# Down projections of a two-layer trunk on one core: shared sums left in PSUM, ScalarE's and the loads' order changed, GpSimd's weight remainders in operations of 256 columns

## Chip, core and metric

One core of one Trainium2 chip. The time is device microseconds of one execution; the kernel before takes 2417.88 us, the median of three runs (2416.55 to 2417.92).

## What is computed

A causal decoder trunk of two layers runs one step over 1024 prompt tokens and 32 sample tokens (1056 columns; activations lie feature by token, 128 features to a tile). Each layer has a mixer (convolution and dilated attention in layer 0, short convolution and spatial gating in layer 1) and a feed-forward part. Only that part is touched:

```python
gu = h @ P['ffn_w_gate_up'][layer]
x = x + mod[:, 5] * ((jax.nn.silu(gu[..., :FFN_HIDDEN]) * gu[..., FFN_HIDDEN:]) @ P['ffn_w_down'][layer])
```

`D_MODEL` is 1024 and `FFN_HIDDEN` 2816, which is eleven groups of 256 hidden features.

## The kernel before

**Operands in two words.** Every float32 operand is split into a high and a low part (`hi`, `lo`, fp32r), and a product is three matmuls: high by high, high by low, low by high. ScalarE makes the high words with a copy, GpSimd the low ones with a subtraction (`raw - hi`), a quarter of a slot of 2048 columns at a time.

**Seven products.** The gate and up projections and most of the down projection are done as 2 by 2 block products with seven multiplications in place of eight. Sums of the blocks are therefore needed of the weights (VectorE, `weight_sums` L2334 to L2340, `words_summed` L2371 to L2376) and of the activations, and the seven products have to be combined afterwards.

**Gate and up (`ffn`, items `split`, `w_split`, `products`).** For each group the gate, then the up unit. ScalarE splits the raw weights (`part_hi`, L1821) and then their sums (`sums_hi`, L1827, one copy of 2048 columns); GpSimd follows with `part_lo` and `sums_lo` (L3075), both waiting on the semaphore `part_hi_done`. During an up unit ScalarE's next work behind `sums_hi` is two copies of product 1 to `f_sum` (`copy_p1`, L1837), for which TensorE waits before it adds the next product into the same bank. What the down projection needs of a group (hidden features and four sums of their blocks) is written to a scratch tensor in HBM.

**Down (`piece_products` L3428, `piece_leaves`).** Group 10 goes first in the plain way, group 9 last (`down_blocks`, L3563), and groups 0 to 8 in five chunks of 1, 2, 2, 2, 2 groups (`CHUNKS`). A chunk has four pieces (one for each pair of output tiles, `m`), a piece two steps (one for each pair of token blocks, `PAIRS`), a step seven products, and a product three matmuls of 264 columns for each group: 21 matmuls a step in chunk 0, 42 in the others. That is 20 pieces a layer. The products of a step lie in four of six PSUM banks (`chain_bank`): chain 0 holds P1, then C11; chain 1 P5, then C12; chain 2 P7, then C21; chain 3 P6. VectorE takes them out in the order P1, P5, P7, P6, C11, C12, C21, and `piece_left` counts these events by seven for each step. P1 + P6 is the shared sum: it is kept in `u_acc` in SBUF over all chunks. In chunk 0 ScalarE copies P1 there (`copy_shared`, L1885), and TensorE waits for that copy (`u_copied`) before product 5, which overwrites the bank; in the other chunks VectorE adds P1 to it (L2414). VectorE adds P6 (L2423). P5 and P7 go straight to x (L2381; L2383 and L2384 for the block that ends in the sample tokens). In the last chunk the whole shared sum is added to x in three places by `add_shared`, half a piece later, reading `u_acc` and x, both in SBUF.

**What feeds a piece.** Each piece has its weights of the chunk's groups (`words`) and their block sums (`word_sums`). In every engine's program order, piece p is preceded by `piece_load` of piece p + 2 (SyncE, L1447), by `piece_words` of piece p + 1 and by one load of an operand of the next chunk (`f_load`, `load_operands`, L1465 to L1468, four of them with `i` = 0 to 3 for two groups, high and low words). `piece_words` is `words_summed` on VectorE, `words_hi` on ScalarE (L1891 for the words, L1893 for the sums) and `words_lo` on GpSimd (L3106, L3108, each one subtraction of 512 columns in chunk 0 and of 1024 in the others). TensorE waits on `word_lo` before products 1 and 2, and at the first piece of a chunk on the operands' loads.

The order of the queues in a piece (`ffn`, from L634):

```python
items.append(Item("piece_load", of=made[p + 2]) if p + 2 < PIECES else Item("last_load", layer=layer, k=p))
...
items.append(Item("piece_words", of=made[p + 1]))
...
elif 0 < piece.chunk < len(CHUNKS) - 1:
    items.append(Item("f_load", layer=layer, chunk=piece.chunk + 1, i=piece.m))
...
items.append(piece)
```

## Time and profile before

| | |
|---|---|
| median of three runs | 2417.88 us |
| the profiled execution, its own time | 2419.25 us |
| its span | 2417.5 us |
| TensorE matmul busy | 2327.5 us (96%) |
| VectorE, ScalarE, GpSimd busy | 1531.6, 799.3, 891.6 us |
| mean granted TensorE clock | 0.991 |
| groups 0 to 8 of the down projection | 1085.33 to 1288.64 us (layer 0), 2167.50 to 2371.92 us (layer 1) |

Busy times of engines are unions of their instructions. PE is TensorE's matmuls and PEld its weight loads; a matmul is recorded with its whole passage, so that consecutive ones overlap, and the distance of their starts is what one costs. DVE is VectorE, ACT ScalarE, POOL GpSimd. "Idle before" is an engine's idle time just ahead of an instruction, with what ended it. A stretch has its start and end, its length, the busy time and number of instructions of PE, PEld, DVE, ACT and POOL, the granted TensorE clock, the DMA engines' busy share and GB/s.

### The profile page before, as it was taken

Reading aid. Unit: us, or ns where it says so; the run is one execution under the profiler, and the core shown is the slowest. Engines: PE = TensorE matmul, PEld = TensorE weight load, DVE = VectorE, ACT = ScalarE, POOL = GpSimd, SP = SyncE. Lnnn points to the kernel's source line nnn. Section 1 sums busy time; section 2 is a strip of 40 time slices with the busy share of each in tenths; the row PEclk is TensorE's granted clock in tenths of the full one; section 3 lists DMA queues with packets and bytes.
Section 4 is the critical chain, followed back from the end, with each engine's and each line's share of the span. In section 5 each row is a group of like instructions: output and inputs, shape, how many; then the busy total and the mean of one; then the engine's idle time right before and its main releaser. Section 6 shows DMA issues by size and latency. Waiting matters only on the chain.

```text
span 2417.5 us, 42723 instructions
## 1 busy us (share of the span) xinstructions
PE 2327.5 (96%) x17575; PEld 2203.9 (91%) x17575; DVE 1531.6 (63%) x3075; ACT 799.3 (33%) x1250; POOL 891.6 (37%) x666
## 2 busy tenths in 40 slices
PE   7999999999999999999999999999999999999998
PEld 5997888588999999998998999999999999999997
DVE  5367743567766766758788320546766666658787
ACT  5212334425433333312214212144533333312113
POOL 3221111213445444534443432132545555424440
PEclk9999999999999999999999999999999999999999
DMA  9424343872456455465651688311334353565651
GB/s 306 168 68 146 114 147 99 291 240 86 142 192 238 162 179 195 153 266 206 237 192 53 217 298 284 114 37 36 134 109 170 114 179 116 187 260 199 227 181 73
DMA packets 220158, 411.70 MB, mean 170 GB/s; under 512 B 9588, under 2 KB 200329, under 8 KB 207934
## 3 DMA queue, kind: packets, MB, share of 16 engines
q1 hardware_dynamic: 206058, 328.53, 39.3%
q0 software_dynamic: 5648, 76.29, 9.0%
q10 hardware_dynamic: 8260, 4.15, 0.6%
q8 instruction: 141, 2.31, 0.4%
q14 instruction: 51, 0.42, 0.1%
HBM read 309.14 MB, written 143.64 MB: 187 GB/s over the span
## 4 chain that ended last, share of the span: by engine, by line
PE 67%; DVE 6%; DMA 2%; ACT 2%; issue 2%; SPq 0%; POOL 0%; ACTq 0%; DVEq 0%
PE ps L3297 15%; PE ps L3428 12%; PE ps L3326 10%; PE ps L3328 9%; PE ps L3327 9%; PE ps L3563 4%; PE ps L3517 3%; DVE x L2381 2%; DMA fa_lo<-scratch_f 1%; DMA w_raw<-in_ffn_w_gate_up 1%; PE ps L3698 1%; PE ps L3586 1%; DMA fb_lo_end<-scratch_f 0%; PE ps L3410 0%; DMA cache_v<-in_cache_b_kv 0%
## 5 line engine op out<-in xcount | busy, mean ns | idle before, releaser
L3297 PE MATMUL ps<-h_hi,w_slot 128*128 128x352 f32 x2112 | 538.0, 328 | 2.9 <-DVE acc_s L2272 1.4
L3297 PEld LDWEIGHTS ps<-h_hi,w_slot 128*128 128x128 f32 x2112 | 370.6, 188 | 22.0 <-issue 18.7
L3326 PE MATMUL ps<-h_hi,w_slot 128*128 128x264 f32 x1280 | 367.1, 287 | 3.9 <-ACT f_sum L1837 2.8
L3327 PE MATMUL ps<-h_lo,w_slot 128*128 128x264 f32 x1280 | 363.6, 284 | 0.0
L3328 PE MATMUL ps<-h_hi,w_slot 128*128 128x264 f32 x1280 | 362.3, 283 | 0.0
L3052 POOL TENSOR_TENSOR w_slot<-w_raw,w_slot 128x512 fp32r<-128x512 f32 x132 | 177.6, 1373 | 482.5 <-ACT w_slot L1655 473.7
L3297 PE MATMUL ps<-h_lo,w_slot 128*128 128x352 f32 x1056 | 339.4, 321 | 0.0
L3075 POOL TENSOR_TENSOR w_slot<-w_sum,w_slot 128x512 fp32r<-128x512 f32 x160 | 221.1, 1414 | 267.6 <-ACT w_slot L1827 267.6
L3066 POOL TENSOR_TENSOR w_slot<-w_raw,w_slot 128x512 fp32r<-128x512 f32 x168 | 226.9, 1384 | 187.0 <-DVE w_sum L2340 99.9
L3326 PE MATMUL ps<-t_hi,w_slot 128*128 128x264 f32 x960 | 274.2, 286 | 0.1
L3328 PE MATMUL ps<-t_hi,w_slot 128*128 128x264 f32 x960 | 272.7, 284 | 0.0
L3327 PE MATMUL ps<-t_low,w_slot 128*128 128x264 f32 x960 | 272.7, 284 | 0.0
L3326 PEld LDWEIGHTS ps<-h_hi,w_slot 128*128 128x128 f32 x1280 | 240.3, 188 | 10.9 <-ACT f_sum L1837 5.3
L3328 PEld LDWEIGHTS ps<-h_hi,w_slot 128*128 128x128 f32 x1280 | 241.2, 188 | 0.0
L3327 PEld LDWEIGHTS ps<-h_lo,w_slot 128*128 128x128 f32 x1280 | 240.7, 188 | 0.0
L3297 PEld LDWEIGHTS ps<-h_lo,w_slot 128*128 128x128 f32 x1056 | 199.5, 189 | 0.1
L3428 PE MATMUL ps<-fa_hi,p_hi 128*128 128x264 f32 x560 | 164.4, 294 | 25.9 <-ACT u_acc L1885 12.0
L3326 PEld LDWEIGHTS ps<-t_hi,w_slot 128*128 128x128 f32 x960 | 180.5, 188 | 5.3 <-issue 4.9
L3328 PEld LDWEIGHTS ps<-t_hi,w_slot 128*128 128x128 f32 x960 | 180.7, 188 | 0.0
L3327 PEld LDWEIGHTS ps<-t_low,w_slot 128*128 128x128 f32 x960 | 180.4, 188 | 0.0
L3106 POOL TENSOR_TENSOR p_lo<-p_raw,p_hi 128x1024 fp32r<-128x1024 f32 (+1 forms) x40 | 87.2, 2180 | 251.3 <-DVE p_raw L2376 251.3
L2381 DVE SCALAR_TENSOR_TENSOR x<-ps,mod,x 128x264 f32<-128x264 f32 x280 | 134.6, 490 | 46.2 <-PE ps L3428 44.3
(460 smaller groups left out, 5181.0 us busy)
## 6 DMA issues: line engine op xcount, KB each, us to landing
w_raw<-in_ada_w SPq DMA_DIRECT2D x48, 1024.0 KB, 6.0
w_raw<-in_ffn_w_gate_up SPq DMA_DIRECT2D x44, 1024.0 KB, 5.2
out_kv_sample<-in_cache_b_kv POOLq DMA_DIRECT2D x8, 4088.0 KB, 22.6
scratch_f<-ft_hi SPq DMA_DIRECT2D x18, 1056.0 KB, 8.6
scratch_f<-ft_lo SPq DMA_DIRECT2D x18, 1056.0 KB, 10.3
fa_hi<-scratch_f SPq DMA_DIRECT2D x10, 1848.0 KB
fa_lo<-scratch_f SPq DMA_DIRECT2D x10, 1848.0 KB
p_raw<-in_ffn_w_down SPq DMA_DIRECT2D x72, 256.0 KB, 3.0
```

Of the source, the lines that this page charges most:

```text
L2381: return dve.scalar_tensor_tensor(x[:, m, c], src, gate, x[:, m, c], ALU.mult, ALU.add)
L3052: pool.tensor_tensor(lo_of(u)[:, c], w_raw[raw_of[u].slot][:, c], hi_of(u).bitcast(F32)[:, c], ALU.subtract)\
L3066: pool.tensor_tensor(w_slot[slot_of(it.raw)][:, c], w_raw[it.raw.slot][:, c], w_slot[it.hi[0]].bitcast(F32)[:, c], ALU.subtract).then_inc( ...
L3075: pool.tensor_tensor(w_slot[it.sums[0]][:, c], whole[:, c], w_slot[it.sums_hi[0]].bitcast(F32)[:, c], ALU.subtract).then_inc(part_made, 1)
L3106: pool.tensor_tensor(p_lo[a][:, c], p_raw[a][:, c], p_hi[a].bitcast(F32)[:, c], ALU.subtract).then_inc(word_lo, 1)
L3297: mm = pe.matmul(big(t)[:, b, 0:BLK], wt, xt[:, k, b * BLK:b * BLK + BLK], start=(k == 0 and n == 0), stop=(k == K - 1 and n == 2))
L3326: pe.matmul(bank(it, j), w_high, x_high, start=first, stop=False, skip_group_check=True)
L3327: pe.matmul(bank(it, j), w_high, x_low, start=False, stop=False, skip_group_check=True)
L3328: return pe.matmul(bank(it, j), w_low, x_high, start=False, stop=last, skip_group_check=True)
L3428: mm = pe.matmul(ps[:, chain_bank(step, chain), 0:QB], w, xt, start=(start and u == 0 and n == 0), stop=(u == U - 1 and n == 2), skip_grou ...
L3517: return pe.matmul(big(t + m)[:, b, 0:BLK], halves[s][:, k, m * P:m * P + P], xt[:, k, b * BLK:b * BLK + BLK], start=(k == 0 and step == 0 ...
L3563: mm = pe.matmul(big(t + i)[:, bank, 0:BLK], halves[s][:, k, m * P:m * P + P], xt[:, k, c], start=(k == 0 and n == 0), stop=(k == 1 and n ...
```

## The change

- In the last chunk VectorE writes P1 + P6 back to the PSUM bank of chain 3 and adds it to x from there in three places, between C11 and C12 of the same step, with two waits on its own earlier results. `add_shared` is gone. The bank is free for TensorE after C12 rather than after P6, and the first tile of `down_blocks` waits for the last of these additions (`u_added`).
- ScalarE in chunk 0: `words_hi` of piece p + 1 stands between the two `copy_shared` of piece p, not ahead of both.
- ScalarE, sums of gate and up weights: two copies of 1024 columns; for an up unit the second stands behind the two copies of product 1. GpSimd's `sums_lo` waits for each half.
- Operand loads of chunks 2 to 4: both of the first group with piece 0 of the chunk before, the third with piece 1, the fourth with piece 2.
- `words_lo` on GpSimd: operations of 256 columns.

```diff
@@ make_plan, ffn
             items.append(Item("products", of=up, which=0))
+            items.append(Item("w_split_rest", of=up))
...
             elif 0 < piece.chunk < len(CHUNKS) - 1:
-                items.append(Item("f_load", layer=layer, chunk=piece.chunk + 1, i=piece.m))
+                for i in ((0, 1), (2,), (3,), ())[piece.m]:
+                    items.append(Item("f_load", layer=layer, chunk=piece.chunk + 1, i=i))
@@ chain_before
-                        return piece_left, 7 * back + LAST_LEFT[other]
+                        in_last = back % (2 * PIECES) >= 2 * (PIECES - 4)
+                        return piece_left, 7 * back + (C12_LEFT if in_last and other == 3 else LAST_LEFT[other])
@@ ScalarE
-                act.activation(w_slot[it.hi[0]], w_raw[it.raw.slot], ACT.Copy).then_inc(part_hi_done, 1)
-
-            def sums_hi(it):
-
+                act.activation(w_slot[it.hi[0]], w_raw[it.raw.slot], ACT.Copy).then_inc(part_hi_done, 2)
+
+            def sums_hi(it, half):
+
+                c = slice(1024 * half, 1024 * half + 1024)
                 act.wait_ge(sums_made, 4 * it.n + 4)
                 act.wait_ge(*it.sums_hi[1])
-                act.activation(w_slot[it.sums_hi[0]], w_sum[it.sums[0]].rearrange("p s k n -> p (s k n)"), ACT.Copy)\
+                act.activation(w_slot[it.sums_hi[0]][:, c], w_sum[it.sums[0]].rearrange("p s k n -> p (s k n)")[:, c], ACT.Copy)\
                     .then_inc(part_hi_done, 1)
...
+            def copy_shared(it, i):
+
+                step = 2 * it.n + i
+                act.wait_ge(piece_done, 7 * step + P1_LEFT)
+                act.activation(u_acc[:, it.m, HALF[PAIRS[i]]], ps[:, chain_bank(step, 0), 0:QB], ACT.Copy).then_inc(u_copied, 1)
...
                 elif it.kind == "w_split":
-                    sums_hi(it.of)
+                    sums_hi(it.of, 0)
+                    if it.of.role == "f_gate":
+                        sums_hi(it.of, 1)
+                elif it.kind == "w_split_rest":
+                    sums_hi(it.of, 1)
...
                 elif it.kind == "piece_words":
-                    words_hi(it.of)
+                    if it.of.k not in range(1, 5):
+                        words_hi(it.of)
                 elif it.kind == "piece":
                     if it.chunk == 0:
-                        copy_shared(it)
+                        copy_shared(it, 0)
+                        words_hi(pieces_of[it.layer][it.k + 1])
+                        copy_shared(it, 1)
@@ VectorE, piece_leaves
-                    dve.tensor_tensor(u, four, u, ALU.add).then_inc(piece_left, 1)
-                    if last and i:
-                        add_shared(it, PAIRS[0])
-                    elif last and it.m:
-                        add_shared(pieces_of[it.layer][it.k - 1], PAIRS[1])
+                    dve.tensor_tensor(four if last else u, four, u, ALU.add).then_inc(piece_left, 1)
                     done(C11_LEFT)
                     add_to_x(m0, B0[r], one_, g0).then_inc(piece_left, 1)
+                    if last:
+                        made(P6_LEFT)
+                        add_to_x(m1, B1[r], four, g1)
+                        add_to_x(m0, B1[r], four, g0)
+                        add_to_x(m1, B0[r], four, g1).then_inc(u_added, 1)
+                        dve.wait_ge(u_added, 8 * it.layer + 2 * it.m + i + 1)
                     done(C12_LEFT)
...
-                if last and it.m == 3:
-                    add_shared(it, PAIRS[1])
@@ GpSimd
-                pool.wait_ge(part_hi_done, it.r + 1)
+                pool.wait_ge(part_hi_done, 2 * it.r + 2)
...
                 for q in range(4):
+                    if q % 2 == 0:
+                        pool.wait_ge(part_hi_done, 2 * it.rs + 1 + q // 2)
...
                 pool.wait_ge(word_sums, 4 * it.n + 4)
-                pool.tensor_tensor(p_lo[a][:, c], p_raw[a][:, c], p_hi[a].bitcast(F32)[:, c], ALU.subtract).then_inc(word_lo, 1)
-                pool.wait_ge(word_hi, 2 * it.n + 2)
-                pool.tensor_tensor(p_lo[b][:, c], p_raw[b][:, c], p_hi[b].bitcast(F32)[:, c], ALU.subtract).then_inc(word_lo, 1)
+                for n, w in enumerate((a, b)):
+                    pool.wait_ge(word_hi, 2 * it.n + 1 + n)
+                    for q in range(2 * len(it.units)):
+                        d = slice(256 * q, 256 * q + 256)
+                        low = pool.tensor_tensor(p_lo[w][:, d], p_raw[w][:, d], p_hi[w].bitcast(F32)[:, d], ALU.subtract)
+                    low.then_inc(word_lo, 1)
@@ TensorE, down_blocks
-                    if it.of.src == "hidden" and i < 2:
-                        pe.wait_ge(piece_left, 7 * (2 * PIECES * (it.of.layer + 1) - 1) + (7 if i else P6_LEFT))
+                    if it.of.src == "hidden" and i == 0:
+                        pe.wait_ge(u_added, 8 * (it.of.layer + 1))
+                    elif it.of.src == "hidden" and i == 1:
+                        pe.wait_ge(piece_left, 14 * PIECES * (it.of.layer + 1))
```

## Rows read from the trace of the kernel before

**Rows 1.** The page: busy time by engine, and the chain that ended last.

```profile
PE 2327.5 (96%) x17575; PEld 2203.9 (91%) x17575; DVE 1531.6 (63%) x3075; ACT 799.3 (33%) x1250; POOL 891.6 (37%) x666
...
PE 67%; DVE 6%; DMA 2%; ACT 2%; issue 2%; SPq 0%; POOL 0%; ACTq 0%; DVEq 0%
```

**Rows 2.** Waits of TensorE's weight loads, whole run: us in total, times, longest.

```profile
PEld ps L3428 <- ACT u_acc L1885: 13.7, 8, 2.5
PEld ps L3428 <- DVE x L2381: 11.9, 6, 2.1
...
PEld ps L3326 <- ACT f_sum L1837: 5.3, 12, 0.4
```

**Rows 3.** Stretches (columns above): chunk 0, chunks 1 to 3, last chunk; then layer 1.

```profile
1085.33:1115.35 30.02, 23.46 (x170) 22.41 (x169) 25.89 (x77) 8.57 (x16) 12.30 (x8) 0.94 0.49 179
1115.35:1239.86 124.51, 123.48 (x1010) 122.97 (x1009) 96.58 (x257) 25.49 (x24) 57.21 (x24) 1.00 0.66 234
1239.86:1288.64 48.78, 43.60 (x337) 42.97 (x338) 44.63 (x106) 8.72 (x8) 21.06 (x12) 0.97 0.32 110
2167.50:2199.10 31.60, 24.94 (x171) 23.89 (x169) 26.48 (x78) 8.56 (x16) 12.27 (x8) 0.89 0.47 171
...
2324.19:2371.92 47.73, 42.24 (x340) 41.40 (x339) 44.98 (x108) 8.71 (x8) 21.10 (x12) 1.00 0.25 91
```

**Rows 4.** The chain that ended last, down projections: start us, us, what.

```profile
1111.53 117.08 PE ps L3428 x954
1229.56 10.26 DMA fa_lo<-scratch_f
...
2273.72 9.38 DMA fb_lo_end<-scratch_f
```

**Rows 5.** Timeline of VectorE and GpSimd in the last chunk of layer 0.

```profile
1254.40 4.05 DVE L2381 SCALAR_TENSOR_TENSOR x<-u_acc,mod,x 128x264 f32<-128x264 f32 x3
...
1288.49 1.29 DVE L2381 SCALAR_TENSOR_TENSOR x<-ps,mod,x 128x264 f32<-128x264 f32 x3
1289.82 1.30 DVE L2381 SCALAR_TENSOR_TENSOR x<-u_acc,mod,x 128x264 f32<-128x264 f32 x3
...
1252.82 2.41 POOL L3106 TENSOR_TENSOR p_lo<-p_raw,p_hi 128x1024 fp32r<-128x1024 f32 x1 [7.09 <-DVE p_raw L2376]
1255.19 2.57 POOL L3108 TENSOR_TENSOR p_lo<-p_raw,p_hi 128x1024 fp32r<-128x1024 f32 x1
```

**Rows 6.** Timeline of ScalarE, VectorE and GpSimd in chunk 0 of layer 0.

```profile
1110.14 1.06 ACT L1893 ACTIVATE p_hi<-p_raw 128x1024 fp32r<-128x1024 f32 x1 [3.21 <-DVE p_raw L2376]
1111.11 0.37 ACT L1885 ACTIVATE u_acc<-ps 128x264 f32<-128x264 f32 x1
...
1109.68 0.43 DVE L2376 TENSOR_TENSOR p_raw<-p_raw,p_raw 128x256 f32<-128x256 f32 x1
...
1110.26 2.38 POOL L3106 TENSOR_TENSOR p_lo<-p_raw,p_hi 128x1024 fp32r<-128x1024 f32 x1 [4.76 <-DVE p_raw L2376]
1112.59 2.41 POOL L3108 TENSOR_TENSOR p_lo<-p_raw,p_hi 128x1024 fp32r<-128x1024 f32 x1
```

**Rows 7.** Groups of GpSimd's subtractions by form: busy us, mean ns of one.

```profile
L3108 POOL TENSOR_TENSOR p_lo<-p_raw,p_hi 128x1024 fp32r<-128x1024 f32 x32 | 77.6, 2425 | 0.0
...
L3108 POOL TENSOR_TENSOR p_lo<-p_raw,p_hi 128x512 fp32r<-128x512 f32 x8 | 10.3, 1287 | 0.0
```

**Rows 8.** Stretch with three operand loads under way (columns as in rows 3).

```profile
1062.00:1082.00 20.00, 19.25 (x118) 18.93 (x119) 12.06 (x28) 2.69 (x5) 2.54 (x2) 1.00 0.87 367
```

**Rows 9.** Timeline of ScalarE and GpSimd in an up unit of layer 1.

```profile
1955.23 1.90 ACT L1827 ACTIVATE w_slot<-w_sum 128x2048 fp32r<-128x2048 f32 x1
1957.04 0.65 ACT L1837 ACTIVATE f_sum<-ps 128x264 f32<-128x264 f32 x2
...
1957.21 5.22 POOL L3075 TENSOR_TENSOR w_slot<-w_sum,w_slot 128x512 fp32r<-128x512 f32 x4 [5.39 <-ACT w_slot L1827]
```

**Rows 10.** A stretch of chunk 0 in layer 1 (columns as in rows 3).

```profile
2171.30:2174.70 3.40, 3.40 (x16) 3.40 (x17) 1.89 (x6) 0.64 (x2) 1.50 (x2) 0.50 0.92 381
```

More of the change, by code:

```diff
@@ L1878, in up_products @@
                             copy_gate_p1(sevens["f_gate", it.layer, it.j + 1], m)
-            def copy_shared(it):
-                for i, r in enumerate(PAIRS):
-                    step = 2 * it.n + i
-                    act.wait_ge(piece_done, 7 * step + P1_LEFT)
-                    act.activation(u_acc[:, it.m, HALF[r]], ps[:, chain_bank(step, 0), 0:QB], ACT.Copy).then_inc(u_copied, 1)
+            def copy_shared(it, i):
+                step = 2 * it.n + i
+                act.wait_ge(piece_done, 7 * step + P1_LEFT)
+                act.activation(u_acc[:, it.m, HALF[PAIRS[i]]], ps[:, chain_bank(step, 0), 0:QB], ACT.Copy).then_inc(u_copied, 1)
             def words_hi(it):
@@ L2384, in add_to_x @@
                 return dve.tensor_tensor(acc_s[:, m, :], src[:, n:n + S_TOK], acc_s[:, m, :], ALU.add)
-            def add_shared(it, r):
-                u = u_acc[:, it.m, HALF[r]]
-                g0, g1 = [mod[:, 6 * it.layer + it.gate, m, 0:1] for m in (2 * it.m, 2 * it.m + 1)]
-                dve.wait_ge(piece_left, 7 * (2 * it.n + PAIRS.index(r)) + C21_LEFT)
-                add_to_x(2 * it.m, B1[r], u, g0)
-                add_to_x(2 * it.m + 1, B1[r], u, g1)
-                add_to_x(2 * it.m + 1, B0[r], u, g1).then_inc(u_added, 1)
             def piece_leaves(it):
@@ L3101, in words_lo @@
             def words_lo(it):
-                a, b, c = it.words[0], it.word_sums[0], slice(0, 512 * len(it.units))
-                pool.wait_ge(word_hi, 2 * it.n + 1)
+                a, b = it.words[0], it.word_sums[0]
                 pool.wait_ge(word_sums, 4 * it.n + 4)
-                pool.tensor_tensor(p_lo[a][:, c], p_raw[a][:, c], p_hi[a].bitcast(F32)[:, c], ALU.subtract).then_inc(word_lo, 1)
-                pool.wait_ge(word_hi, 2 * it.n + 2)
-                pool.tensor_tensor(p_lo[b][:, c], p_raw[b][:, c], p_hi[b].bitcast(F32)[:, c], ALU.subtract).then_inc(word_lo, 1)
+                for n, w in enumerate((a, b)):
[4 more added lines that the diff above has]
+                    low.then_inc(word_lo, 1)
             moved = [0]
```

1 line of the change is left out of this document (removed).

## Prediction, made before the changed kernel was timed

> **What bounds the kernel.** I read the page first. TensorE's matmuls are busy 96% of the span and hold 67% of the chain that ended last [rows 1]. So an edit pays only where TensorE itself waits, and the next view is the list of its waits [rows 2]. Three of the longest are in the lines of this change: product 5 of chunk 0 waits for ScalarE's copy of P1 (13.7 us, 8 times), steps of the last chunk wait for VectorE's additions to x (11.9 us, 6 times), and the up units wait for ScalarE's copy to `f_sum` (5.3 us, 12 times).
>
> A list of waits counts some idle time that is no loss, so I measure against distances. Undisturbed, 954 matmuls of L3428 take 117.08 us [rows 4], 0.1227 us each with two short waits inside; I use 0.122. A step of 42 matmuls is then 5.12 us, a two-group piece 10.25, a one-group piece 5.12. The stretches [rows 3] say where more is taken. Chunks 1 to 3 are nearly clean (124.51 us for 1008 matmuls, which make 123.0). Chunk 0 has 168 matmuls, 20.5 us, and takes 30.02 and 31.60. The last chunk has 336, 41.0 us, and takes 48.78 and 47.73. These stages are where the time lies.
>
> **1. Shared sum in PSUM, last chunk.** Three additions of `u_acc` to x take 4.05 us while GpSimd's two subtractions of 1024 columns run, and 1.30 us when GpSimd is idle [rows 5]. The last of the three ends 0.7 us behind GpSimd: additions with both inputs in SBUF stand still beside it. Additions to x from PSUM do not: three take 1.29 us [rows 5]. There are three such groups in each layer, and three TensorE waits of 1.8 to 2.1 us behind them. With the source in PSUM I expect none of it, that is 7.8 us back in layer 0 (48.78 less 41.0) and 6.7 in layer 1, 14.5 in all; 1.5 of layer 0's is the lower clock behind such a wait (granted 0.97 over 48.78 us [rows 3]).
>
> What is put in: the same number of additions, now all between C11 and C12. The write of P1 + P6 goes to PSUM, which no row shows; I take the 0.43 us it has now. The wait for P6 is hidden by C11. The wait on `u_added` lets one addition end before the next starts, 0.49 in place of 0.40 us: 0.09 a step. VectorE's work in the chunk: 44.6 us busy [rows 3], less three groups of about 2.8 us standing still (8.8 with the longer third), plus the group of 1.3 us that now falls behind the end, plus eight waits of 0.09 = 37.8 us, against TensorE's 41.0. It fits, but not in every step. From a step's start, by 0.73 us a product and 0.2 until VectorE begins: P6 is in `four` at 3.5, C11 added at 4.25, the shared sum at 5.5, C12 and C21 at 6.3. Then come the next piece's four block sums (0.43 us each, some 0.36 in a row [rows 6]) until 7.8, and P1, which TensorE needs at 5.12 + 2.93 = 8.05, has left at about 8.2: 0.2 us, three times a layer, 1.2 in all. The bank of chain 3, now free after C12, is asked for more than a step later: no cost, and still none if C12 came 2 us late. The first tile of L3563 wants the last three additions at 5.12 and gets them at about 5.6: 0.5 a layer, 1.0 in all. With 0.3 for rests, the part gives **12.0 us**.
>
> The Trainium skill, VectorE: DVE Perf Modes, section "The TRN2 errata — SBUF-src ops pay a fixed extra latency per instruction", gives VectorE 58 cycles and the columns for an SBUF source and 120 for a PSUM source, at 0.96 GHz: 65 ns more for each addition that now reads PSUM. By that 48 additions would cost 3.1 us of VectorE, and this part would give about 10. The trace disagrees: 1.29 us for three from PSUM, 1.30 for three from SBUF.
>
> **2. ScalarE's order in chunk 0.** ScalarE does the high words of the next piece's sums, which wait for VectorE, before it copies P1: in piece 3, 1.06 us, and TensorE is held until 1111.5 [rows 6]. The copy needs only P1. With it ahead, that wait goes; the second copy has the words between (2 x 0.6 us), and is needed 4 us after the piece starts, so it is on time. Late next is VectorE. It is busy 25.89 of 30.02 us in chunk 0, 26.48 of 31.60 in layer 1 [rows 3], more than TensorE's 20.5, and the same work stays. I take its work as the new length, 26.0 and 26.5: 4.0 and 5.1 us back. The granted clock is 0.94 and 0.89 here [rows 3]: stretches of 3.4 us at 0.50, once in layer 0 and twice in layer 1 [rows 10], each behind a wait of TensorE. One costs up to 1.7 us, some 1.2 where VectorE sets the pace. TensorE still waits in piece 0, so I leave one in: minus 1.2.
>
> **3. GpSimd in 256 columns.** 1024 columns take 2.42 us and 512 take 1.29 [rows 7]: 2.2 ns a column and 0.15 fixed, so 256 take about 0.72, 0.70 in a row. Eight are 5.6 us where two were 4.75. A piece of 10.25 us hides that. Not so at piece 4, the first with 1024 columns behind a short piece: GpSimd starts at 1110.26 behind VectorE's sums and ends at 1115.00 [rows 6]; TensorE needs it at 1115.35 + 0.73. Of this 1.1 us spare the longer subtractions take 0.85, and part 2 takes about 1.1 more, since piece 3 itself shortens by its 2.4 us wait while VectorE's queue gives 1.3 back. That is 0.9 us of new wait a layer, 1.8 in all. Bounds for one operation: 0.62 (half of a 512 in a row) and 1.25 (as long as a 512). At 0.62 the wait is 0.3; at 1.25 see the third rival. Parts 2 and 3 together: 9.1 - 1.2 - 1.8 = **6.1 us**.
>
> **4. Loads.** The fourth load of a chunk is issued with the last piece and lands 10.3 and 9.4 us later [rows 4], a piece being 10.25: TensorE waits 1.2 us twice and 0.8 once. One piece earlier, none is left: **3.2 us**. Moved with it: SyncE issues two loads of 1.85 MB at piece 0, and the next words' loads queue behind them. With three under way 367 GB/s came in [rows 8], so 3.7 MB are there in 10 us, as the next piece's words are issued; those are needed a piece later. No cost; if they came at the 184 GB/s of a lone load (1.85 MB in 10.3 us), see the second rival.
>
> **5. Sums of gate and up weights in halves.** The 1.90 us copy ends at 1957.13 and the `f_sum` copies start only then [rows 9]. Half the copy is about 1.0, so they start 0.9 earlier, more than any of the 12 waits (0.4 at most [rows 2]): all go. The 5.3 us are idle time of the weight loads, which run a little ahead of their matmuls, and so an upper end; the lower is nothing; I take **4.5**. The second half ends at about 1958.6, GpSimd has the first two quarters until 1958.9 (5.22 us for four): not delayed. Splitting costs ScalarE 0.1 us each time; it is busy 33% of the span [rows 1]. Gate units gain nothing that TensorE waits for.
>
> **Sum.** 12.0 + 6.1 + 3.2 + 4.5 = 25.8 us. The profiled execution took 2419.25, so 2393.4; it lies 1.37 above the median, so in terms of the median 2392.1: **2392 us**, 1.1% less.
>
> **Rivals.**
> - **VectorE becomes the bound of the last chunk.** Ten operations a step leave it 3 us of 41 spare. Suppose the write to PSUM and the two waits keep the four operations from overlapping at all: 4 x 0.09 us in 16 steps, 5.8 us, or the 65 ns of part 1. It would have less than nothing to spare behind the block sums, and 4 to 6 of the 12 us are not had: 2396 to 2398. For it: its margin, and the order, which puts 1.2 us ahead of C12. Against: it catches up in every second step. 12%. The skill's rule alone: 2394.
> - **The words come late.** If two operand loads hold back the words for pieces 2 of chunks 1 to 3 by 2.5 us each, six times, 15 us are lost: 2407. Against: rows 8. 4%.
> - **Slower: GpSimd becomes the bound of the pieces.** Its eight subtractions must fit between VectorE's block sums (1 us after a piece starts) and product 2 of the next (11.0 us): from 1.24 us for one on, each 0.1 us more costs 0.8 us in each of 32 pieces, 25.6. At 1.24 itself the chunk ends already lose 13 us in chunk 0 and 7 in the last chunk (2411); at 1.29 the kernel is at 2423, slower. Against: rows 7 put one at 0.7, and the fixed part would have to be seven times what they show. 3%.
> - **More is had.** VectorE waits for TensorE in part of chunk 0, its queue shortens, no lower clock is left: 2386 to 2389. 9%.
>
> My forecast, 2389 to 2396, has the other 72%. About 0.2% (5 us) is what a measurement can tell from no change here. The range reaches into the first rival and the fourth: 2385 to 2402. Faster by over 0.2%: 0.94; within: 0.03, where several parts fail together; slower: 0.03.
>
> **What would show it.** Right: no L3428 waits for ScalarE's `u_acc` copy; x additions in the last chunk of 0.49 us at most, the chunk at 42 us; chunk 0 near 27 us with VectorE as releaser and one wait for GpSimd's `p_lo` at piece 4; no operand load among the waits; subtractions of 256 columns near 0.72 us. Wrong: these above 1.2 us; the last chunk over 45 us with `u_acc` or x as releaser; `p_raw` loads ahead of TensorE's waits; VectorE's block sums standing still more often beside GpSimd than before.

## The result, and the profile after

The changed kernel takes 2384.95 us (median of 4 runs, 2384.13 to 2385.49) against 2417.9 for the kernel before on the same chip: the ratio is 0.9855 [0.9829, 0.9881]. 32.9 us are gone where 25.8 were forecast. The time lies 0.05 us below the low end of the range, which is less than the four runs differ among themselves; the gain was forecast with the right sign and too small. The profiled execution took 2385.49 us, its span is 2383.7, against 2417.5 before: 33.8 us between the spans.

The page after, beside [rows 1]: busy time by engine, then the chain that ended last.

```profile
PE 2315.9 (97%) x17575; PEld 2194.3 (92%) x17575; DVE 1512.2 (63%) x3075; ACT 807.2 (34%) x1290; POOL 934.7 (39%) x874
...
PE 73%; DVE 4%; issue 1%; ACT 1%; POOL 0%; ACTq 0%; DVEq 0%
```

TensorE has the same matmuls, and 73% of the chain in place of 67%. VectorE's share fell from 6% to 4%, and the loads (DMA 2% before) have left the chain. GpSimd is busy 43 us longer in 208 more operations, and its share of the chain stays at 0%.

Waits of TensorE's weight loads in the down projections of layer 0 after (us in total, times, longest), beside [rows 2]:

```profile
PEld ps L3432 <- DVE acc_s L2394: 4.1, 8, 1.2
PEld ps L3432 <- POOL p_lo L3111: 0.8, 1, 0.8
...
PEld ps L3432 <- DVE u_acc L2415: 0.7, 2, 0.3
```

The waits for ScalarE's `u_acc` copy and for VectorE's additions of `u_acc` to x are gone, and so are those for the operand loads. Left are chunk 0, where the sixth and the seventh product of each piece's first step wait for VectorE, four times each; piece 4, which waits once for GpSimd's low words; and two waits of 0.3 us for P1 in the last chunk (L2415).

Stretches after, columns as in [rows 3]: chunk 0, chunks 1 to 3 and last chunk of layer 0, then the same of layer 1.

```profile
1082.02:1108.08 26.06, 23.10 (x171) 21.19 (x170) 24.89 (x77) 9.54 (x17) 12.63 (x19) 1.00 0.58 207
1108.08:1231.78 123.70, 123.12 (x1011) 122.91 (x1010) 95.91 (x254) 25.39 (x24) 68.93 (x99) 1.00 0.64 236
1231.78:1274.23 42.45, 41.68 (x339) 41.08 (x337) 38.85 (x112) 9.03 (x9) 22.96 (x30) 1.00 0.35 126
...
2145.60:2171.67 26.07, 23.06 (x170) 21.14 (x169) 24.90 (x77) 9.55 (x17) 12.65 (x19) 1.00 0.57 207
2171.67:2295.38 123.71, 123.16 (x1011) 122.94 (x1010) 95.91 (x254) 25.52 (x24) 68.93 (x99) 1.00 0.65 236
2295.38:2337.92 42.54, 41.68 (x339) 41.07 (x337) 38.95 (x112) 8.60 (x8) 23.00 (x30) 1.00 0.28 102
```

And the stage ahead of them, gate and up, with group 10 at its end: first the two layers before, then the two after.

```profile
619.44:1085.34 465.90, 462.14 (x3867) 445.06 (x3866) 312.77 (x532) 167.74 (x217) 220.29 (x162) 1.00 0.56 193
1726.01:2167.50 441.49, 437.12 (x3505) 433.48 (x3505) 287.17 (x492) 162.10 (x197) 218.31 (x162) 1.00 0.44 159
```

```profile
619.21:1082.02 462.81, 461.05 (x3865) 444.62 (x3865) 304.72 (x532) 170.78 (x236) 221.46 (x164) 1.00 0.56 195
1711.22:2145.60 434.38, 432.40 (x3507) 431.37 (x3505) 295.79 (x492) 165.33 (x216) 232.55 (x164) 1.00 0.45 162
```

So the 33.8 us, by stage, both layers (every length runs between TensorE's first matmuls of two stages; the last chunks of [rows 3] end one matmul later, and by this measure they are 48.62 and 47.57 us long before):

| stage | forecast | between the profiles |
|---|---|---|
| last chunk | 12.0 | 11.2 (6.17 + 5.03) |
| chunk 0 and chunks 1 to 3 | 9.3 | 11.7 (9.5 and 2.2) |
| gate and up, without group 10 | 4.5 | 7.4 (2.11 + 5.31) |
| group 10 of gate and up | 0 | 2.8 (0.97 + 1.81) |
| all else | 0 | 0.7 |

A step to compare with [rows 5], with GpSimd at work beside it, is the first of the last chunk in layer 0. Timeline of VectorE after, and of GpSimd beside it (start us, us, what):

```profile
1235.32 0.43 DVE L2424 TENSOR_TENSOR ps<-ps,u_acc 128x264 f32<-128x264 f32 x1
1235.65 0.49 DVE L2391 SCALAR_TENSOR_TENSOR x<-ps,mod,x 128x264 f32<-128x264 f32 x1
1236.06 0.45 DVE L2393 SCALAR_TENSOR_TENSOR x<-ps,mod,x 128x232 f32<-128x232 f32 x1
...
1234.01 5.64 POOL L3111 TENSOR_TENSOR p_lo<-p_raw,p_hi 128x256 fp32r<-128x256 f32 x8 [4.61 <-DVE p_raw L2386]
```

The sum into PSUM (L2424), which no row of before showed, takes 0.43 us, as was assumed. The additions behind it take 0.45 to 0.49 us each while GpSimd's eight subtractions run. None of them stands still.

### The profile page after: what moved, and what is told of

Its sections match the earlier page's. It is cut to its first block, busy times and chain, and to the rows that moved or that the text cites. A ratio compares the mean times of both kernels' runs of the same rounds, so it can differ in the third digit from the quotient of the medians.

```text
span 2383.7 us, 43027 instructions
## 1 busy us (share of the span) xinstructions
PE 2315.9 (97%) x17575; PEld 2194.3 (92%) x17575; DVE 1512.2 (63%) x3075; ACT 807.2 (34%) x1290; POOL 934.7 (39%) x874
## 4 chain that ended last, share of the span: by engine, by line
PE 73%; DVE 4%; issue 1%; ACT 1%; POOL 0%; ACTq 0%; DVEq 0%
PE ps L3301 15%; PE ps L3432 14%; PE ps L3330 11%; PE ps L3331 11%; PE ps L3332 11%; PE ps L3569 4%; PE ps L3521 3%; PE ps L3704 1%; PE ps L3592 1%; DVE x L2391 0%; PE ps L3898 0%; POOL p_lo L3111 0%; PE ps L3414 0%; PE ps L3739 0%; DVE x L2191 0%
## 5 line engine op out<-in xcount | busy, mean ns | idle before, releaser
L3077 POOL TENSOR_TENSOR w_slot<-w_sum,w_slot 128x512 fp32r<-128x512 f32 x160 | 234.7, 1495 | 244.2 <-ACT w_slot L1831 244.2
L3111 POOL TENSOR_TENSOR p_lo<-p_raw,p_hi 128x256 fp32r<-128x256 f32 x288 | 202.6, 742 | 202.5 <-DVE p_raw L2386 202.5
L2391 DVE SCALAR_TENSOR_TENSOR x<-ps,mod,x 128x264 f32<-128x264 f32 x312 | 148.0, 489 | 40.9 <-PE ps L3432 38.8
```

Source lines behind the costliest of these rows:

```text
L2391: return dve.scalar_tensor_tensor(x[:, m, c], src, gate, x[:, m, c], ALU.mult, ALU.add)
L3077: pool.tensor_tensor(w_slot[it.sums[0]][:, c], whole[:, c], w_slot[it.sums_hi[0]].bitcast(F32)[:, c], ALU.subtract).then_inc(part_made, 1)
L3111: low = pool.tensor_tensor(p_lo[w][:, d], p_raw[w][:, d], p_hi[w].bitcast(F32)[:, d], ALU.subtract)
```

## The experiments

Kernels named "before +" are the kernel before with one part of the diff alone; kernels named "after" are the changed one with one edit, or with two or three where the name says "both". Each was timed beside the kernel before on the same chip, on three chips in all. The kernel before has a median of 2420.25 us beside "before + halves", "+ PSUM sum", "+ 256 columns" and "after, source in SBUF", and 2417.15 to 2418.47 beside the rest, so times of different chips are compared by their ratios.

My theory was that each part acts in its own stage by the wait that the forecast names. Against it stood that the 256-column operations alone free the last chunk, so that the PSUM sum adds nothing; that the new order, and not the source, is what counts there; and, for the surplus, that it is chance between executions.

### One part at a time

**Before + halves** (part 5 of the diff, whole: two copies of 1024 columns, the second one of an up unit behind the copies of product 1, and GpSimd waiting for each half; one line of it is shown):

```diff
-                act.activation(w_slot[it.sums_hi[0]], w_sum[...])
+                act.activation(w_slot[it.sums_hi[0]][:, c], w_sum[...][:, c])
```

> The kernel before with part 5 alone (gate and up weights' sums copied by ScalarE in halves, GpSimd waiting for each half). My recorded term was 4.5 us. Theory A (the waits were undersized): each wait for the f_sum copy also delays the matmul behind it, about 0.50 us in place of 0.38, and the stretch at the lower clock ahead of group 10 in layer 1 (1.7 us) goes with them; the gate and up stretches of both layers together shorten by 9 to 10 us, as they do between the two full kernels, so 2408 to 2409. Theory B (the excess comes from another part): this kernel gives 4 to 5 us, 2413. Rival to both: the clock stretch stays, 2410.

Measured: 2410.88 us (2406.66 to 2413.24, 8 runs), ratio 0.996 [0.9945, 0.9975]. Gate and up without group 10 are 1.96 and 4.99 us shorter. With this part alone, then, 7.0 of the 7.4 us are had. That is more than the 5.3 us of all the waits that I had called the upper end. With group 10 the two stages are 6.5 us shorter and not the 9 to 10 that theory A wants: the stretch at the lower clock in group 10 of layer 1 stayed (26.62 us long at a granted clock of 0.94), as the expectation's rival has it. Stretches of gate and up without group 10 (layers 0 and 1; before they are 440.60 and 415.36 us):

```profile
619.29:1057.94 438.65, 437.32 (x3722) 421.79 (x3721) 288.48 (x498) 168.03 (x232) 218.62 (x160) 1.00 0.55 188
1725.11:2135.48 410.37, 408.81 (x3362) 408.41 (x3361) 281.80 (x460) 162.72 (x212) 229.33 (x160) 1.00 0.43 152
```

**Before + PSUM sum** (part 1, whole: the sum in PSUM, its three additions in the new place, and the later release of the bank; one line is shown):

```diff
-                    dve.tensor_tensor(u, four, u, ALU.add).then_inc(piece_left, 1)
+                    dve.tensor_tensor(four if last else u, four, u, ALU.add).then_inc(piece_left, 1)
```

> The kernel before with the shared sum in PSUM alone, GpSimd's subtractions still of 1024 columns. If the source in SBUF is what stood still, the last chunk falls from 48.6 and 47.6 us to the 42.5 of the full change in both layers, 11 us in all: 2406 to 2407. If the 256-column operations did part of it, the last chunk stays above 44 us: 2409 or more.

Measured: 2406.2 us (2403.84 to 2408.11, 6 runs), 0.9942 [0.9925, 0.996]. Last chunks:

```profile
1243.86:1286.31 42.45, 41.68 (x338) 41.08 (x337) 38.85 (x112) 9.03 (x9) 20.38 (x12) 1.00 0.35 126
...
2316.44:2358.90 42.46, 41.69 (x339) 41.08 (x337) 38.85 (x112) 8.61 (x8) 20.41 (x12) 1.00 0.28 102
```

Alone it gives the whole of the last chunk, with GpSimd still in 1024 columns. The last chunks are 11.3 us shorter, and the median is 14.1 lower. The rest must lie in stages that the edit doesn't touch; that it is the clock isn't shown, but this profile has one stretch at the lower clock behind 600 us, and that of before has five.

**Before + 256 columns** (part 3):

```diff
+                    for q in range(2 * len(it.units)):
+                        d = slice(256 * q, 256 * q + 256)
```

> The kernel before with GpSimd's low words in operations of 256 columns alone. A VectorE addition with both inputs in SBUF stands still until the GpSimd operation under way ends, and gets in before the next one. With operations of 0.74 us the three additions then take about 2.5 us in place of 4.05, and TensorE's waits in the last chunk shrink to some 0.5 us each: last chunk 44 to 46 us. Piece 4 of each layer waits little, since chunk 0 still runs at ScalarE's pace. 2411 to 2414. If instead VectorE gets in only when GpSimd is wholly done, the last chunk grows by some 0.8 us a group: 2419 to 2421. If the split only costs, without a gain: 2418 to 2420.

Measured: 2411.5 us (2404.64 to 2415.17, 9 runs), 0.9961 [0.9947, 0.9974]. Last chunk of layer 0, and its three additions of `u_acc` that took 4.05 us [rows 5]:

```profile
1242.42:1287.01 44.59, 42.05 (x339) 41.21 (x338) 41.84 (x107) 8.71 (x8) 24.42 (x30) 1.00 0.34 120
```

```profile
1256.86 2.56 DVE L2381 SCALAR_TENSOR_TENSOR x<-u_acc,mod,x 128x264 f32<-128x264 f32 x3
```

So the short operations alone win 4.0 and 3.0 us in the last chunks: the three additions end at 1257.64, 1258.53 and 1259.42 us, each 0.3 behind the end of one of GpSimd's subtractions (1257.36, 1258.24, 1259.13), and a subtraction that nothing holds up is now 0.74 us long. It is a second cure of the same illness, and the weaker one. Beside the PSUM sum nothing is left for it: 42.45 us with it and without.

**After, source in SBUF** (the new order of the last chunk, but P1 + P6 goes to `u_acc`):

```diff
-                    dve.tensor_tensor(four if last else u, four, u, ALU.add).then_inc(piece_left, 1)
+                    dve.tensor_tensor(u, four, u, ALU.add).then_inc(piece_left, 1)
-                        add_to_x(m1, B1[r], four, g1)
+                        add_to_x(m1, B1[r], u, g1)
```

> The changed kernel, but P1 + P6 of the last chunk is written to u_acc in SBUF and added from there, in the new place between C11 and C12. Order, waits and 256-column operations stay. If the source is what matters, additions from SBUF run beside GpSimd's operations and each stands still up to 0.74 us: TensorE waits come back in the last chunk, 1 to 2 us a piece in pieces 16 to 19, 2389 to 2394. If the new place and the short operations are what heals it, the time stays within 1 us of the changed kernel: 2385.

Measured: 2405.59 us (2401.91 to 2408.04, 6 runs), 0.9939 [0.9922, 0.9956]. I had expected 2389 to 2394; it is worse. The last chunks take 50.2 and 50.5 us, longer than before the change. The stretch in layer 0, and VectorE in one step with GpSimd beside it:

```profile
1234.16:1284.37 50.21, 42.86 (x338) 41.40 (x337) 48.34 (x112) 9.19 (x9) 24.29 (x30) 1.00 0.30 107
```

```profile
1237.22 0.46 DVE L2393 SCALAR_TENSOR_TENSOR x<-ps,mod,x 128x232 f32<-128x232 f32 x1
...
1240.06 0.99 DVE L2393 SCALAR_TENSOR_TENSOR x<-u_acc,mod,x 128x232 f32<-128x232 f32 x1
1240.97 0.72 DVE L2394 TENSOR_TENSOR acc_s<-u_acc,acc_s 128x32 f32<-128x32 f32 x1
1241.62 1.00 DVE L2391 SCALAR_TENSOR_TENSOR x<-u_acc,mod,x 128x264 f32<-128x264 f32 x1
...
1236.39 5.94 POOL L3111 TENSOR_TENSOR p_lo<-p_raw,p_hi 128x256 fp32r<-128x256 f32 x8 [4.61 <-DVE p_raw L2386]
```

GpSimd's eight subtractions run until 1242.33. Beside them an addition from SBUF takes 1.0 us, one from PSUM 0.46, and even 32 columns from SBUF take 0.72. VectorE is busy 48.3 of the 50.2 us, and TensorE's 336 matmuls need 41.0: VectorE is the bound. The new order puts every shared addition beside GpSimd's work, so it is good only with the PSUM source. This is the strongest test of part 1's mechanism, as the place of the sum is all that differs. The Trainium skill, SBUF — State Buffer, section "Who interferes with whom", says that a VectorE instruction with two SBUF inputs contends with a GpSimd instruction that reads SBUF, and one with at most one SBUF input, outside VectorE's two-port modes, does not. All rows here agree.

**Before + order** (part 2), **before + loads** (part 4):

```diff
-                        copy_shared(it)
+                        copy_shared(it, 0)
+                        words_hi(pieces_of[it.layer][it.k + 1])
+                        copy_shared(it, 1)
```

> The kernel before with ScalarE's order in chunk 0 alone (copy of P1, then the next words, then the second copy). Chunk 0 falls from 30.0 to 31.6 us to 26.0, VectorE's own work, in both layers, with TensorE's waits now before products 5 and 6 behind VectorE; piece 4 waits for GpSimd at most 0.2 us with operations of 1024 columns: 8 to 9.5 us faster in the two chunks. Rival: the next piece's words, now later on ScalarE, hold GpSimd and then TensorE: chunk 0 at 27 us or more, or a wait at pieces 1 to 4 for p_lo.

Measured: 2413.11 us (2406.81 to 2417.72, 11 runs), 0.9976 [0.9964, 0.9987]. That is 5.1 us less by the medians where 8 to 9.5 were expected, though chunk 0 is as short as expected. Chunk 0 in the two layers:

```profile
1089.29:1115.31 26.02, 23.03 (x170) 21.13 (x169) 24.86 (x77) 9.54 (x17) 11.71 (x8) 1.00 0.57 207
...
2165.84:2191.93 26.09, 23.10 (x170) 21.19 (x170) 24.93 (x77) 9.54 (x17) 11.73 (x8) 1.00 0.57 207
```

Between the profiles the two chunks are 9.5 us shorter, and the spans differ by 6.1. Much of the 9.5 is the clock: the profile before has three stretches of the lower clock in chunk 0 and this one has none, but it has two in places where before had none (group 10 of layer 0, 26.60 us at 0.94, and the last chunk of layer 1). The old order at the full clock is seen in layer 1 of "before + PSUM sum", and the same 28.68 us in layer 1 of "before + loads":

```profile
2163.93:2192.61 28.68, 22.01 (x170) 20.93 (x169) 25.70 (x77) 8.57 (x16) 12.30 (x8) 1.00 0.52 188
```

So the order itself is worth 2.6 us a layer, and a stretch of the lower clock in chunk 0 costs 1.3 to 1.5 us more.

```diff
+                for i in ((0, 1), (2,), (3,), ())[piece.m]:
+                    items.append(Item("f_load", layer=layer, chunk=piece.chunk + 1, i=i))
```

> The kernel before with the operand loads of chunks 2 to 4 one piece earlier, alone. The waits for fa_lo and fb_lo_end at chunk starts (1.2, 1.2 and 0.8 us in the profile before) go, chunks 1 to 3 fall to 123.7 us where the clock is full, 2.2 us in all in the profile; p_raw's landings get later at the second piece of a chunk, without a wait of TensorE. Rival: a p_raw that lands late holds VectorE's block sums and TensorE waits at the third piece of a chunk.

Measured: 2416.12 us (2414.74 to 2421.91, 11 runs), 0.999 [0.9979, 1.0]; chunks 1 to 3 take 122.88 and 122.94 us, before 124.51 and 125.09.

```profile
1119.43:1242.32 122.89, 122.89 (x1011) 122.89 (x1010) 95.17 (x253) 25.49 (x24) 57.18 (x24) 1.00 0.64 237
```

TensorE is busy in all of this stretch. By stage the loads give 3.8 us (3.2 forecast). The medians show 2.0, and the interval reaches from 0 to 5 us: too small an effect for these runs.

Added up, the five parts alone save 14.1 + 9.4 + 8.8 + 5.1 + 2.0 = 39.3 us by the medians (from unrounded times), together 32.9. The 7.0 us of the last chunk that PSUM sum and short operations both claim are in it twice; without them it is 32.3. The agreement is no better than the medians are: each of the five has an interval of 2.5 to 4.2 us to either side.

### What bounds what is left

**After, shorter P5** (the addition of P5 in chunk 0 cut to 32 columns, so that its other columns are missing from x):

```diff
-                    add_to_x(m1, B1[r], two, g1).then_inc(piece_left, 1 if it.chunk else 2)
+                    c5 = B1[r] if it.chunk else slice(B1[r].start, B1[r].start + 32)
+                    add_to_x(m1, c5, two if it.chunk else two[:, 0:32], g1).then_inc(piece_left, 1 if it.chunk else 2)
```

> The changed kernel with VectorE's addition of P5 in chunk 0 cut to 32 of 264 columns (the other columns' share of x is left out), the same operation and events. If VectorE's work sets chunk 0's length, each of eight additions a layer gives back about 0.3 us: 26.05 falls to 23.5 to 24 us. If it is ScalarE, GpSimd or the order of events, it stays above 25.5.

Measured: 2387.53 us (2381.14 to 2391.41, 4 runs), 0.9867 [0.9848, 0.9887]. Chunk 0 falls from 26.06 to 24.26 us, and VectorE's busy time in it from 24.89 to 22.95:

```profile
1082.04:1106.30 24.26, 22.82 (x169) 20.95 (x169) 22.95 (x74) 9.54 (x17) 12.27 (x18) 1.00 0.61 222
```

Taking 1.9 us from VectorE takes 1.8 us from the chunk (a little less than was expected), so VectorE's work is its length, as part 2 has it. The stage behind gives 0.6 of it back: chunks 1 to 3 take 124.29 and 124.26 us in place of 123.70.

**After, whole low-word operations** (1024 or 512 columns again, the rest as after):

```diff
-                    for q in range(2 * len(it.units)):
-                        d = slice(256 * q, 256 * q + 256)
-                        low = pool.tensor_tensor(p_lo[w][:, d], p_raw[w][:, d], p_hi[w].bitcast(F32)[:, d], ALU.subtract)
+                pool.tensor_tensor(p_lo[a][:, c], p_raw[a][:, c], p_hi[a].bitcast(F32)[:, c], ALU.subtract).then_inc(word_lo, 1)
```

> The changed kernel with GpSimd's low words in one operation of 512 or 1024 columns again. If the shared sum from PSUM no longer cares for GpSimd, the last chunk stays at 42.5 us, and the wait at piece 4 for p_lo (0.84 us a layer, behind eight operations of 0.70 us) shrinks to at most 0.2: 1.3 to 1.7 us faster than the changed kernel. If the short operations still help VectorE's block sums, which have both inputs in SBUF, chunk 0 or the last chunk grows by over 0.5 us and the time stays the same or rises.

Measured: 2385.49 us (2382.52 to 2392.34, 5 runs), 0.9861 [0.9839, 0.9884]. Chunks 1 to 3 take 122.93 and 122.94 us against 123.70 and 123.71, and the last chunk is unchanged (42.45 and 42.48 us):

```profile
1112.75:1235.68 122.93, 122.93 (x1010) 122.92 (x1009) 95.42 (x254) 25.51 (x24) 57.82 (x25) 1.00 0.64 237
```

So in company, part 3 costs 0.77 us a layer, which is the wait at piece 4 (0.9 forecast), and buys nothing.

**After, P1 first** (in the last chunk, P1 leaves ahead of the next piece's block sums; part 1 forecast 0.2 us for that wait, three times a layer):

```diff
+                    if last and i == 0 and it.k + 1 < PIECES:
+                        words_summed(pieces_of[it.layer][it.k + 1])
...
-                    words_summed(it.of)
+                    if it.of.k <= PIECES - 4:
+                        words_summed(it.of)
```

> The changed kernel, but in the last chunk VectorE adds P1 of a piece's first step ahead of the next piece's block sums. The 0.4 us that TensorE waits before product 5 in pieces 17 and 18 goes: 0.8 us a layer, last chunk 41.7 us, 1.5 us faster. If VectorE's work as a whole, not its order, sets the chunk, the wait moves to product 6 or 7 and nothing is won.

Measured: 2389.21 us (2386.62 to 2391.6, 4 runs), 0.9875 [0.9857, 0.9894]. The last chunks take 41.93 and 42.01 us, 0.5 less each (0.8 expected). In the median nothing of it shows against the unedited kernel, run next:

```profile
1234.13:1276.06 41.93, 41.41 (x339) 41.09 (x337) 38.80 (x112) 8.91 (x9) 22.92 (x30) 1.00 0.35 128
```

**After again** (no edit, to see what repeats):

> The changed kernel once more, beside its variants: 2383 to 2387. If the lower clock is granted where TensorE has waited, this kernel, whose longest wait behind the start of layer 0's feed-forward part is 1.2 us, shows at most one such stretch between 600 us and its end, and its runs lie closer together than those of the kernel before (2412 to 2426 on the last chip).

Measured: 2389.17 us (2388.22 to 2389.82, 4 runs), 0.9875 [0.9858, 0.9892]. Two parts of the expectation failed: it lies above 2387, and it has two stretches of the lower clock behind 600 us, not one. The third held: its runs lie within 1.6 us. The two sets of runs of one and the same program don't overlap. They were taken at different times and perhaps on different chips; but the kernel with whole low-word operations spreads from 2382.5 to 2392.3 on this chip by itself. Of 4.4 us between the spans, 4.2 lie in group 10 of gate and up (24.32 us twice after, 26.74 and 26.15 here). Group 10 of layer 0, after and after again:

```profile
1057.70:1082.02 24.32, 23.58 (x144) 22.96 (x145) 14.76 (x33) 2.45 (x4) 2.83 (x4) 1.00 0.79 323
```

```profile
1057.21:1083.95 26.74, 25.22 (x144) 24.64 (x145) 15.49 (x35) 2.44 (x4) 2.84 (x4) 0.94 0.71 294
```

and VectorE and GpSimd shortly ahead of it, after and then after again:

```profile
1050.93 0.71 DVE L2323 TENSOR_TENSOR tmp<-f_sum,tmp 128x528 f32<-128x528 f32 x1
...
1050.94 1.86 POOL L3067 TENSOR_TENSOR w_slot<-w_raw,w_slot 128x512 fp32r<-128x512 f32 x1 [7.58 <-ACT w_slot L1824]
```

```profile
1050.22 1.66 DVE L2323 TENSOR_TENSOR tmp<-f_sum,tmp 128x528 f32<-128x528 f32 x1
...
1050.04 1.28 POOL L3067 TENSOR_TENSOR w_slot<-w_raw,w_slot 128x512 fp32r<-128x512 f32 x1 [7.39 <-ACT w_slot L1824]
```

After, VectorE starts 0.01 us ahead of GpSimd and takes 0.71 us, while GpSimd's subtraction takes 1.86. In the other run GpSimd is 0.18 us ahead and takes 1.28 us, and VectorE takes 1.66. GpSimd works on weights that ScalarE copies as soon as their load lands, and that copy starts at 1048.04 us here against 1048.94. TensorE's second wait in the group (for `f_sum`) then makes a matmul start 1.18 us behind the one ahead, not 0.40, and soon behind it comes a stretch at the lower clock (granted 0.94 over the 26.74 us). Here an earlier transfer goes with a longer stage.

The other profiles bear this out. Fourteen of the sixteen kernels profiled leave group 10 and GpSimd's subtractions for it as they were, which makes 28 such stages (all but the last two below):

| first of the two | stages | VectorE's operation | group 10 |
|---|---|---|---|
| VectorE | 8 | 0.71 us | 24.32 to 24.57 us, none with a stretch of lower clock |
| GpSimd | 8 | 1.36 to 1.82 us | 25.07 to 25.35 us at the full clock |
| GpSimd | 12 | 1.22 to 1.82 us | 25.97 to 26.77 us with a stretch of lower clock |

So the order is worth about 0.8 us, and only in the longer order does a stretch of lower clock follow, for about 1.3 us more. The order isn't wholly chance either: in the five kernels without part 5 GpSimd was first in all ten stages, and in the nine with part 5 VectorE was first in 8 of 18. In the profile before GpSimd leads by 0.44 and 0.63 us, with part 5 alone by 0.02 twice. That part 5 brings VectorE forward to the tie fits this, but no run tests it.

### A better version

**After, both** (whole operations and P1 first), twice:

> Both: whole subtractions on GpSimd and P1 ahead of the block sums. If the two are independent, 3 us faster than the changed kernel.

Measured: 2385.16 us (2383.3 to 2387.51, 4 runs), 0.9859 [0.9841, 0.9878].

> The combined version once more (whole subtractions for the words, P1 ahead of the block sums), as the base of the two beside it: 2383 to 2388. Group 10's stage, ahead of chunk 0, comes out at 24.3 to 24.6 us where VectorE's product of the hidden features (L2323) starts ahead of GpSimd's subtraction of the down weights (L3067), and at 25.2 to 26.8 where GpSimd starts first.

Measured: 2389.36 us (2382.46 to 2391.26, 5 runs), 0.9883 [0.9862, 0.9903]. By stages it is better than the changed kernel in both layers: chunks 1 to 3 122.96 and 122.96 us, last chunks 41.92 and 42.01, together 2.6 us less. Its profiled span is 2380.7 us against 2383.7. The timed runs don't tell the two kernels apart, since group 10 alone moves by 4 us from profile to profile. In the other profile of this kernel (span 2385.8 us) these stages are as short, while group 10 took 26.73 and 24.57 us.

**Both, and GpSimd held behind VectorE** (to fix the order ahead of group 10):

```diff
+                else:
+                    pool.wait_ge(hidden_made, 4 * (sevens["f_up", it.layer, GROUPS - 1].n // 2) + 1)
```

> The combined version, with GpSimd's low words of group 10's down weights held until VectorE's first product of the last up unit (L2323) is done. If the two lengths of group 10's stage come from who takes the read path first, it is 24.3 to 24.7 us in both layers in this kernel, with no wait of TensorE for f_sum above 0.3 us, and the runs lie 1 to 3 us lower than the base's and closer together. If the landing of the weights itself or the clock makes the two lengths, both still occur, at 24.3 and at 25.2 to 26.8; if TensorE then waits for GpSimd in place of VectorE, it is 25 us or more in every run.

Measured: 2385.24 us (2381.76 to 2387.09, 4 runs), 0.9862 [0.9841, 0.9883]. Group 10 in both layers:

```profile
1059.35:1083.67 24.32, 23.58 (x145) 22.96 (x145) 14.75 (x33) 2.44 (x4) 2.56 (x2) 1.00 0.78 323
...
2122.16:2146.65 24.49, 23.73 (x144) 23.13 (x145) 14.43 (x31) 2.44 (x4) 2.54 (x2) 1.00 0.78 320
```

**Both, and those GpSimd operations in 256 columns:**

```diff
-                for q in range(4):
-                    c = slice(512 * q, 512 * q + 512)
+                w = 512 if it.kind == "seven" else 256
+                for q in range(2048 // w):
+                    c = slice(w * q, w * q + w)
```

> The combined version, with the low words of group 10's down weights in operations of 256 columns (two for each event). VectorE's operation then stands at most 0.74 us beside GpSimd in place of 1.3: TensorE's wait for f_sum shrinks from 1.0 to 0.5 us or less, that for f_lo (0.83 us) to 0.3 to 0.6. GpSimd itself takes 0.7 us longer. If standing still sets the stage: 24.0 to 25.0 us; if GpSimd's length does: 25 us or more.

Measured: 2385.92 us (2381.25 to 2388.63, 4 runs), 0.9865 [0.9842, 0.9888]. Group 10 takes 23.03 us and 23.26, the shortest of all, but the stretch with what lies ahead of it is the same as without the edit, here first, and both at the granted clock of 1.00 (24.0 to 25.0 had been expected for group 10):

```profile
620.03:1082.46 462.43, 460.49 (x3866) 444.74 (x3866) 303.66 (x532) 170.68 (x236) 222.85 (x166) 1.00 0.56 195
```

```profile
618.82:1081.23 462.41, 460.88 (x3865) 444.60 (x3865) 303.29 (x532) 170.83 (x236) 221.58 (x162) 1.00 0.56 195
```

The 1.3 us are lost ahead of group 10: GpSimd's subtractions take 7.65 us there in place of 6.69, and TensorE waits for them 1.53 us before the group's first matmul in place of 0.76. Neither edit beats the changed kernel by what the runs can tell. Holding GpSimd back keeps group 10 short in both layers of one profile (24.32 and 24.49) and costs 0.5 and 0.3 us ahead of it; that it does so in every run isn't shown.

## Why the prediction was right in its sign and too small

- **Part 1, right.** 12.0 forecast, 11.2 measured, both from the PSUM source and from nothing else (42.45 us with this part alone, 50.2 without it). VectorE needs 38.9 us of the chunk's 42.5 (37.8 taken). The wait for P1 was told as 0.2 us three times; it is 0.3 us twice by the list, and 0.5 us a layer when taken away. The wait of the first tile behind the chunk, 0.5 us a layer in the sum, is 0.7 and 0.8. Another 0.3 us of what is missing is no cost: the last chunks were measured one matmul too long. The first rival, VectorE as the bound, is what happens with the SBUF source only.
- **Part 2, right in mechanism, a little low.** 7.9 forecast, 9.5 measured. The copy's wait is gone and VectorE's work is the length of chunk 0: 26.0 and 26.5 us taken, 26.06 and 26.07 measured, and 1.8 us shorter when VectorE is given less. The 1.2 us that I took off for a stretch of lower clock was not due: the clock stays at 1.00 in chunk 0, here and in every kernel with this part. Its size was about right (1.3 to 1.5 us measured). Three such stretches make 4.3 of the 9.5 us, and they were in the profile before; the order alone gives 5.2.
- **Part 3, right as a price, silent on its overlap.** One subtraction takes 0.742 us (0.72 taken). Group after, columns as in [rows 7]:

```profile
L3111 POOL TENSOR_TENSOR p_lo<-p_raw,p_hi 128x256 fp32r<-128x256 f32 x288 | 202.6, 742 | 202.5 <-DVE p_raw L2386 202.5
```

  The new wait at piece 4 is 0.77 us a layer (0.9 taken). That the same edit alone would win 7 us in the last chunk stands nowhere in the forecast. It did not matter for the sum, as part 1 had all of it already.
- **Part 4, right:** 3.2 forecast, 3.8 measured by stage, and with this part alone TensorE has no wait left in chunks 1 to 3.
- **Part 5 is the step that failed.** I wrote that the 5.3 us of waits are "an upper end" and took 4.5; it gave 7.4 (7.0 alone). Two reasons. First, a wait of the weight loads was not an upper end. In layer 1 before, the list has 10 waits for `f_sum` of 0.44 us each, and the stage is 5.3 us shorter without them. Starts of TensorE's matmuls at one of them:

```profile
1956.95 0.28 PE L3328 MATMUL ps<-h_hi,w_slot 128*128 128x264 f32 x1
1957.46 0.39 PE L3326 MATMUL ps<-h_hi,w_slot 128*128 128x264 f32 x1 [0.23 <-ACT f_sum L1837]
1957.69 0.28 PE L3327 MATMUL ps<-h_lo,w_slot 128*128 128x264 f32 x1
1957.81 0.28 PE L3328 MATMUL ps<-h_hi,w_slot 128*128 128x264 f32 x1
```

The matmul behind the wait starts 0.51 us after the one ahead, and the next one 0.23 after it, where undisturbed both distances are 0.12: 0.50 us for each wait, 5.0 of the 5.3, against the 0.38 taken. Second, I wrote that "gate units gain nothing that TensorE waits for". In layer 0 before, four waits for the gate's copies (1.9 us) stand in the list beside two for `f_sum` (0.9); after, 0.7 us of these is left, and the stage is 2.1 us shorter. The kernel with this part alone shows the same (1.96 us); why the gate's copies come earlier with it stays open. Waits of the weight loads in layer 0 before, and after:

```profile
PEld ps L3326 <- ACT tmp L1837: 1.0, 2, 0.5
...
PEld ps L3326 <- ACT tmp_x L1837: 0.9, 2, 0.5
PEld ps L3326 <- ACT f_sum L1837: 0.9, 2, 0.4
```

```profile
PEld ps L3330 <- ACT tmp L1841: 0.5, 1, 0.5
PEld ps L3330 <- ACT tmp_x L1841: 0.2, 1, 0.2
```

- **Not counted at all: group 10**, 2.8 us between the two profiles. No line of it is changed. It falls into one of two orders by a fraction of a microsecond, and in the profile after it had the shorter one in both layers; after again had the longer. How much of this is part 5's doing and how much chance isn't shown.
- **The surplus, then:** 33.8 less 25.8 is 8.0 us between the spans. Part 5 is 2.9 of it, group 10 2.8, chunk 0 1.6 (1.2 of these the clock allowance), chunks 1 to 3 0.8, the rest 0.7, and part 1 takes 0.8 back. Of these only group 10 changes sign between executions: after again, 1.4 us longer than before in group 10, has a surplus of 3.6. Its median of 2389.17 us would have lain inside the range. So a gain above 25.8 us is shown, and that it went past the end of the range is in part luck with group 10.
- The rival "more is had" (2386 to 2389, 9%) names the end that came true, and half of its condition holds: no lower clock was left in chunk 0, but VectorE's work still sets the chunk's length. GpSimd as the bound, the slower rival, didn't come: at 0.742 us a subtraction is far from its 1.24.

## What to carry to other kernels

Where one engine's step stands still beside another's, ask which operand ties them, and move that operand, before shortening the other engine's operations: here PSUM in place of SBUF gave 11.2 us, and 256 columns in place of 1024 gave 7.0 alone and nothing on top. A list of waits gives neither an upper end nor the whole list of gainers: look up every wait that the moved instruction's own engine releases in the stage, and price each with the matmul behind it. And measure an effect of 2 to 4 us by stages of the profile when one untouched stage moves by 4 us between executions.

## What the runs showed of the hardware that I had not expected

- VectorE gets in between two GpSimd operations that follow each other without a gap: three additions from SBUF take 4.05 us beside operations of 1024 columns [rows 5] and 2.56 beside those of 256. The Trainium skill, SBUF — State Buffer, section "Who interferes with whom", says that issue order, not op shape, decides who blocks. The rows ahead of group 10 agree: with VectorE first its operation took 0.71 us and GpSimd's 1.86, with GpSimd first 1.66 and 1.28.
- An order settled by as little as 0.01 us in an untouched stage moves it by 0.8 us a layer, and by about 2 with the stretch of lower clock that can follow.
- Stretches of lower clock, 3.4 us at 0.5 [rows 10], come behind waits of TensorE, but not behind each. Before, the profile has five behind 600 us (the last 5 us of each profile left out), in group 10, chunk 0 and the last chunk; after, none; after again, two, both at group 10. From 28.68 us for chunk 0, 47.57 for the last chunk and 25.3 for group 10 at the full clock, I estimate that the five cost 6 of the 33.8 us. What decides between two equal waits isn't settled.
- A read or write in PSUM costs VectorE about what one in SBUF costs with GpSimd idle: 0.44 us for a sum into PSUM against 0.42 into SBUF, 0.49 for an addition from PSUM against 0.48 from SBUF.
